# Expert weights as plain fp32, in a ring of nine whole 2 MB blocks

## The reference

```python
group_prob = softmax(x2 @ w_r1 + b_r1); gp, gi = top_k(group_prob, 1)        # 1 of 4 groups
ev, ei = top_k(sel, 2)                                                        # 2 of its 8 experts
gates = gp * softmax(ev); experts = gi * 8 + ei
...
hid = jax.nn.silu(xblk @ w_gate[e]) * (xblk @ w_up[e])     # [1024, 512] each
return hid @ w_down[e]                                     # [512, 1024]
...
y = segment_sum(rows * row_gate, row_tok)                  # back to the tokens, residual add follows
```

## Time and profile before

| | us |
|---|---|
| median of 3 runs (lowest, highest) | 1799.54 (1798.51, 1801.36) |
| span of the profiled execution | 1797.7 |
| PE, PEld, DVE, ACT, POOL busy in it | 1749.8, 1178.3, 1315.6, 1027.7, 230.2 |
| layer 0's experts, first gate product to last down product's end | 276.9 to 798.0 |
| layer 1's experts, the same | 1259.5 to 1775.7 |

### The profile page before, as it was taken

The page is one execution under the profiler, slowest core; times in us unless marked ns, Lnnn a source line. Parts: engine busy times, 40 slices in busy tenths (PEclk is TensorE's granted clock), DMA queues, the critical chain, the costliest instruction groups (busy, mean ns, idle before and its releaser), DMA issues.

```text
span 1797.7 us, 21881 instructions
## 1 busy us (share of the span) xinstructions
PE 1749.8 (97%) x7712; PEld 1178.3 (66%) x7719; DVE 1315.6 (73%) x1370; ACT 1027.7 (57%) x1067; POOL 230.2 (13%) x136
## 2 busy tenths in 40 slices
PE   8999998999999999999999999999899999999997
PEld 6876786565555555657787777878566665555564
DVE  4999767888888888875443533456988888888887
ACT  4225636777777777763221222233777777777774
POOL 0030001122221222100000000000122122221220
PEclk9999999999999999999999999999999999999999
DMA  8521056999999999995212221213999999999995
GB/s 285 188 94 48 13 199 242 400 408 406 408 405 399 400 402 399 400 358 180 92 50 94 94 94 47 94 69 116 356 403 409 414 407 406 411 404 400 410 388 223
DMA packets 101507, 494.99 MB, mean 275 GB/s; under 512 B 14153, under 2 KB 26441, under 8 KB 52160
## 3 DMA queue, kind: packets, MB, share of 16 engines
q1 hardware_dynamic: 88192, 467.69, 66.3%
q0 software_dynamic: 10176, 16.24, 2.7%
q10 hardware_dynamic: 3072, 10.18, 1.6%
HBM read 484.66 MB, written 26.74 MB: 284 GB/s over the span
## 4 chain that ended last, share of the span: by engine, by line
PE 52%; DMA 26%; DVE 12%; ACT 6%; issue 2%; SPq 1%; DVEq 0%; ACTq 0%
DMA raw<-in_expert_w_gate 26%; PE psum L927 8%; PE psum L928 8%; PE psum L929 8%; DVE w_lo L736 6%; ACT w_hi L749 5%; PE psum L1076 4%; PE psum L1010 4%; PE psum L1007 3%; PE psum L1460 2%; DVE xs L1947 2%; PE psum L1086 1%; PE psum L1091 1%; PE psum L1087 1%; PE psum L1028 1%
## 5 line engine op out<-in xcount | busy, mean ns | idle before, releaser
L736 DVE TENSOR_TENSOR w_lo<-raw,w_hi 128x2048 fp32r<-128x2048 f32 x290 | 663.0, 2288 | 164.0 <-ACT w_hi L749 157.1
L749 ACT ACTIVATE w_hi<-raw 128x2048 fp32r<-128x2048 f32 x290 | 552.3, 1911 | 215.7 <-DMA raw<-in_expert_w_up 88.5
L1010 PE MATMUL psum<-w_lo,uT_hi 128*64 128x512 f32 x992 | 270.8, 395 | 8.5 <-DVE w_lo L736 6.1
L714 ACT ACTIVATE w_hi<-raw 128x2048 fp32r<-128x2048 f32 x46 | 88.1, 1914 | 329.7 <-PE psum L929 329.5
L722 DVE TENSOR_TENSOR w_lo<-raw,w_hi 128x2048 fp32r<-128x2048 f32 x46 | 105.4, 2291 | 200.1 <-ACT w_hi L714 200.1
L1007 PE MATMUL psum<-w_hi,uT_hi 128*128 128x512 f32 x868 | 247.2, 401 | 1.7 <-DVE uT_hi L2226 1.7
L2560 POOL DMA_INDIRECT y_dram<-y_e,index x60 | 120.2, 2003 | 775.0 <-DVE y_e L2261 761.8
L1010 PEld LDWEIGHTS psum<-w_lo,uT_hi 128*64 128x64 f32 x992 | 130.8, 135 | 101.1 <-DVE w_lo L736 23.1
L1007 PEld LDWEIGHTS psum<-w_hi,uT_hi 128*128 128x128 f32 x868 | 160.5, 191 | 41.4 <-DVE uT_hi L2226 2.3
L2555 POOL DMA_INDIRECT x_e<-xs_dram,index x64 | 93.7, 1464 | 656.8 <-DVE index L2221 620.8
L927 PE MATMUL psum<-w_hi,uT_hi 128*128 128x512 f32 x352 | 139.1, 395 | 2.4 <-DVE h L2437 1.4
(11 more groups left out here) (272 smaller groups left out, 2523.5 us busy)
## 6 DMA issues: line engine op xcount, KB each, us to landing
raw<-in_expert_w_gate SPq DMA_DIRECT2D x128, 1024.0 KB
raw<-in_expert_w_up SPq DMA_DIRECT2D x128, 1024.0 KB
raw<-in_expert_w_down SPq DMA_DIRECT2D x68, 1024.0 KB
xs<-in_expert_w_down SPq DMA_DIRECT2D x60, 1024.0 KB, 14.2
raw<-in_odd_w_in SPq DMA_DIRECT2D x8, 2048.0 KB
raw<-in_odd_w_in SPq DMA_DIRECT2D x8, 1024.0 KB
raw<-in_odd_w_out SPq DMA_DIRECT2D x4, 2048.0 KB
raw<-in_even_w_in SPq DMA_DIRECT2D x3, 2048.0 KB
```

What stands on the lines that cost most here:

```text
L736: nc.vector.tensor_tensor(part(w_lo[b]), src, part(w_hi[b]).bitcast(F32), ALU.subtract).then_inc(m.lo[b], 1)
L749: nc.scalar.activation(part(w_hi[b]), src, ACT.Copy).then_inc(m.hi[b], 1)
L1010: mm = nc.tensor.matmul(psum[0:FIRST, bank], xeT_hi[:, 8 * b + 4 * half + j, 0:FIRST], lo[:, j], start=False, stop=False)
```

## The change

Expert weights are no longer split; the gate, up and down products are plain fp32 from the loaded block. Since an expert has at most 64 rows, each product is made in two column halves (`half_width`, `down_half_width`): the first half of the output columns goes to PSUM partitions 0 to 63, the second to 64 to 127, with the same 64 stationary columns. Only the step `BIG` (now 16) uses 128 rows (`full_width`). `copy_tokens`, `copy_hidden` and `hidden` shrink to one instruction each; the hidden rows are turned with two transposes instead of four. The space of the split buffers joins the loaded blocks: nine blocks of 2 MB in a ring (`ring`), three experts deep. Each is one DMA with one semaphore, and PE waits for it whole. Down weights are read as four rows of 4 KB a partition (before: 8 KB pieces), gate and up as 16 KB. SP issues block n + 9 when PE has finished with block n (`gate_psum`, `up_psum`, `down_psum`); blocks 0 to 8 of a layer are issued when their places fall free (`ring_free`). The first odd block is issued after the first two pairs of `y_back` instead of ahead of them. The last two experts' rows are added from partitions 0 to 63 and 64 to 127 for the two column halves (`last_rows`).

```diff
-BIG = STEPS - 3
+EARLY = 3
+BIG = 16
+RING = 3 * EARLY
...
-        wd_dram = expert_w_down.rearrange("l e (p j) n -> l e p (j n)", j=HC)
+        wd_dram = expert_w_down.rearrange("l e (j p) n -> l e p j n", j=HC)
...
+        ring = [[raw[1], raw[2], free_a, raw[0], in_pair[1], free_b, in_pair[0], in_uT, xs],
+                [raw[2], raw[0], free_a, raw[1], in_uT, free_b, in_pair[0], in_pair[1], xs]]
...
+            def half_width(x, w, bank, ready, done):
+
+                for j in range(KC):
+                    if j % 4 == 0:
+                        ready(j // 4)
+                    for c in range(2):
+                        mm = nc.tensor.matmul(psum[c * FIRST:(c + 1) * FIRST, bank, 0:HID // 2], x[:, j, 0:FIRST],
+                                              w[:, j, c * HID // 2:(c + 1) * HID // 2], start=(j == 0), stop=(j == KC - 1))
+                mm.then_inc(done, 1)
...
+            def ring_free(layer, n):
+
+                if n == RING - 1:
+                    sp.wait_ge(xs_stored, 16 * (layer + 1))
+                    full_bank("norm", 2 * layer + 1, TILES - 1, 1)
+                elif not layer:
+                    if n in (0, 1, 3):
+                        sp.wait_ge(lo_ok[1], first_odd - 2 + (0, 1, None, 2)[n])
+                    elif n in (2, 5):
+                        sp.wait_ge(pv_done, TILES * A_HEADS)
+                        sp.wait_ge(csum, 6)
+                    elif n == 6:
+                        sp.wait_ge(*half_used(first_odd - 1, 0))
+                    else:
+                        full_bank("out0", 1, TILES - 1)
...
+                        n = 3 * e + kind
+                        if n < RING:
+                            ring_free(layer, n)
+                        else:
+                            sp.wait_ge((m.gate_psum, m.up_psum, m.down_psum)[kind], past + e - EARLY + 1)
+                        w = ring[layer][n % RING]
+                        dst = w if kind < 2 else chunks_of(w, HC)
+                        sp.dma_start(dst, one(src, layer, at)).then_inc(ring_landed[n % RING], 16)
...
+                def ready_of(n):
+
+                    def ready(half):
+                        if not half:
+                            pe.wait_ge(ring_landed[n % RING], ring_at(layer, n))
+                    return ready
...
+                for e in range(STEPS):
+                    if e:
+                        turned(e - 1)
+                    product = full_width if e == BIG else half_width
+                    pe.wait_ge(m.xT_ok, past + e + 1)
+                    product(xeT[:, e % 2], weights(3 * e, KC), 2, ready_of(3 * e), m.gate_psum)
+                    product(xeT[:, e % 2], weights(3 * e + 1, KC), 3, ready_of(3 * e + 1), m.up_psum)
+                    if e < STEPS - 1:
+                        pe.wait_ge(m.gathered[(e + 1) % 2], 16 * times(layer, e + 1))
+                        transpose_tokens(m, x_e[:, (e + 1) % 2], max(rows_in_step(e + 1), TURN_ROWS))
+                    if e:
+                        down(e - 1)
```

937 lines of the change are left out of this document (301 added, 636 removed).

## The result

The changed kernel takes 1776.14 us (median of 4 runs, 1773.19 to 1780.0), the kernel before beside it 1800.16: ratio 0.987 [0.985, 0.989], 24 us or 1.3% faster. The forecast was 1741.6, a gain of 58: the sign and the mechanism came out, the size did not. The profiled execution took 1773.28 us with a span of 1771.5; the forecast for the span was 1739.8, so 31.7 us have to be found.

A forecast was written before the change was run, and what follows sets the result against it. Transfers bound the expert phases, PE close behind. First product at 276.9, +19.8, +467.2, +1.5; layer 1 from 1233.2, +19.8, +458.4, +1.5, then the end: span 1739.8, +1.8 makes 1741.6 us. Range 1720 to 1778.

The forecast's parts named there:

- What bounds the kernel: Expert phases: transfers end the wait in a steady step (16.49 us layer 0, 16.18 layer 1), PE right behind.
- Part 1: PE's expert products without the split: column halves run side by side, 3.44 us a block, 11.6 us a step.
- A: Rival on PE's expert products, chance 0.09: column halves run in turn, a step is 21.9 us, time about 2164.
- B: Rival on PE's expert products, chance 0.04: halves partly side by side, steps of 16.6 to 20.5 us, time 1765 to 2010.
- E: Rival on PE's weight loads, chance 0.02: loads for a column strip are exposed, a step is 22.8 us, time 2222.
- C: Rival at the start of each phase, chance 0.02: only five blocks land before the first product, time 1775.
- Part 2: Start of each phase: nine blocks begun ahead, layer 0's first gate product stays at about 277, range 0 to 5 us.
- T later than 280: Sign of being wrong: T, layer 0's first gate product, comes after 280 because prefetch is in the gather's way.
- Part 3: Transfers of the remaining 85 blocks keep the old rates: 467.2 us in layer 0, 458.4 in layer 1, +1.5 for landing.
- D: Rival on down transfers, chance 0.12: 4 KB rows cost 10% more, +0.5 us a step, +29, time 1770.
- Part 4: Awaiting whole blocks holds PE back by half a block (2.6 us) once, at the end; all else hides under DMA.
- From the first addition on: DVE's chain from L+4.5 (L: last block's landing) is unchanged, so layer 1's first product comes 26.3 us earlier.

The follow-up runs named there:

- e4_in_turn: Changed kernel with passes reordered, all chunks of the first column half, then all of the second: 1951.71 us, ratio 1.084 to the kernel before.
- e1: Changed kernel with blocks 4 to 7 of layer 0 begun only when the normed tokens are stored: 1772.62 us, ratio 0.984 to the kernel before.
- e10: Changed kernel with blocks 4 to 8 of layer 0 begun only when the first gather has landed: 1779.0 us, ratio 0.988 to the kernel before.
- e11: Changed kernel with at most two ring blocks outstanding beside the one being begun: 1771.62 us, ratio 0.984 to the kernel before.
- e3: Changed kernel with down weights read in pieces of 8 KB instead of 4 KB: 1769.93 us, ratio 0.982 to the kernel before.
- e6_halves: Changed kernel with each ring block begun as two transfers of 1 MB, awaited one by one: 1770.16 us, ratio 0.984 to the kernel before.
- e5_between: Changed kernel with the previous expert's down product made between gate and up instead of behind up: 1766.82 us, ratio 0.981 to the kernel before.
- e2: Changed kernel with the first odd block begun right behind the last expert block: 1775.66 us, ratio 0.986 to the kernel before.

## Why the prediction was right, and where it failed

**What bounds the kernel; the mechanism.** Right. The split's work is gone from DVE and ACT, PE fell below the transfers, the DMA share is 1.01 and 1.02 in the middle of both phases. The time lies inside the stated range of 1720 to 1778, near its upper end: what came is what had been put into the range (late starts, dearer pieces) and at nothing in the sum, and the tail, which stood in neither.

**Part 1, side by side.** Right: 3.67 us a block for a forecast 3.44 (pairs of passes start 0.217 us apart, 15 times that is 3.25, and the last pair's modelled end is 0.42 behind), and e4_in_turn shows that the pairing is what gives it. The argument from attention's row strips carried over to column strips. Rivals A, B and E did not come; A's price of 21.9 us a step was too high in the form that was tried, 18.45. C did not come either: the last of the nine blocks landed at 283.4, ahead of the first product.

**Part 2, the start of layer 0: the step that failed first.** The forecast reckoned with bytes: 10.5 MB and 2.1 MB at 400 GB/s are over by 275. They were over at 284, 9 us later, since the last block waits for the store; and the forecast put the store, which everything waits for, at no place within that sum. Four blocks were begun 5 us ahead of it, and it took 22.6 us instead of 7.5, then the gather was late as well. "The gather may be up to 3 us late; I count nothing" should have been: a short transfer on the path that is begun behind 8 MB of others lands with them. It was +10.1 us, 8.9 of them shown by e1 and e10 to be this contention, against a range of 0 to 5. The prediction's own signs of being wrong named it ("T later than 280"); its sum did not. By a sentence of the Trainium skill (DMA: Bandwidth & Descriptors, Queues, rings and completion order), each engine goes round between its queues, packet by packet; if equal turns moved equal bytes, the store on ACT's queue would have taken about 2 x 7.5 = 15 us, an estimate, and the row shows 22.6. The store goes in pieces of 4 KB beside the blocks' 16 KB, so its turns may have moved fewer bytes; no run here tells.
The release of block 2, behind which SP issues block 11, was placed 1 to 2 us too early (T + 19.8, measured 21.6 and 20.8, by these issues of SP), and the 5 us gap of DMA ahead of it was foreseen:

```profile
308.64 0.38 SPq L765 DMA_DIRECT2D free_a<-in_expert_w_down  x1
...
1273.34 0.38 SPq L765 DMA_DIRECT2D free_a<-in_expert_w_down  x1
```

In layer 0 the granted clock, 0.70 from 284 to 292 behind PE's wait of 8.8 us, has a part in it: the first 64 passes took 7.96 us, 7.13 in layer 1. But the 8 us gap ahead, from 284 to 292, was not in the sum as a loss. It need not have been if T had stayed at 277.

**Part 3, the rate.** The rate was right within 1% in layer 0; in layer 1 it is 1% below the old one (402 for 407 in equal windows). Two terms were missing. First, the tail: 16 us at a share of 0.71 is 4.8 us of idle engines in each layer, which the kernel before has not (0.98); e11 shows its cause. Second, the price of the 4 KB pieces: the forecast had it at most at 0.1 us a step and counted nothing; e3 shows 0.17 and 0.22 us a step, 5 and 6 us a layer, D at a third to two fifths of its price. From block 11's issue at 1273.34 to the landing of the last up block at 1738.78 (PE's row below) lie 84 blocks and 465.4 us, where the forecast has 84 x 5.39 + 1.5 = 454.5; less the tail, 6.1 us are left, 0.22 a step. In layer 0 (308.64 to 775.32) it is 466.7 for 463.2: less the tail, 1.3 us under the forecast. Both layers have the same 16.4 us a step now, where I carried over 16.49 and 16.18. The 6.1 us of layer 1 are about what the lower rate makes (1.2% of 460 us are 5.5), and e3's pieces of 8 KB bring that rate back to 406. Why the kernel before was faster in layer 1 (407) than in layer 0 (403), and this one and e3 are not, stays open.

```profile
1738.78 3.67 PE L911 MATMUL psum<-in_uT,xeT 128*64 128x256 f32 x32 [1.29 <-DMA in_uT<-in_expert_w_up]
```

For layer 1 the account is: block 11 +1.0, tail +4.8, steps +6.1, products behind the last landing +0.8, together 12.7 of the 12.8 us late. For layer 0: block 11 +1.8, tail +4.8, steps -1.3, and the first addition 1.2 us nearer to the last up block's landing than the forecast had it: 4.1 of 4.1.

**Part 4, whole blocks.** Right in kind: e6_halves gained at the ends of the phases (1.5 us a layer) and nothing in the steps. Not in the sum: the clock. Behind PE's waits of 1.6 and 3.6 us a block took 5.1 to 5.3 us; where PE waits for the next block anyway this costs nothing; at a layer's end it does (e5_between).

**From the first addition on.** The forecast called the chain behind it "DVE's own and unchanged" and put the odd block near L + 11. The block did land at 791, L + 11; but it was the change that had put it behind rows of y, and ACT waited 2.2 us for it, with its norm and DVE's reciprocal behind. Before, the reciprocal came 8.8 us behind the first addition, now 11.8. 5.2 us, of which e2 gave 4 back in its profile.

**The end.** Right within 0.4 us.

In one sentence: the forecast was right on what each engine would cost and wrong in taking the transfers as one sum, since some 22 of the missing 32 us (10.1 at the start, 9.6 in the tails, 2.8 of block 11) are DMA engines that stood idle or carried the wrong bytes first; the 4 KB pieces and the late odd block are most of the rest.
